# Table rows of chunk 0 loaded in the projection, its tables made on VectorE, and the last yc store awaited in the recurrence

## What is computed

```python
def decay_matrix(G):
    c = G.shape[-1]
    mask = jnp.tril(jnp.ones((c, c), bool))
    return jnp.exp(jnp.where(mask, G[..., :, None] - G[..., None, :], -jnp.inf))
# gdn_chunked
    A = jnp.eye(c) + jnp.einsum('bnhid,bnhjd->bnhij', kb, k) * dec * strict
    qk = jnp.einsum('bnhid,bnhjd->bnhij', q, k) * dec
# ssd_chunked
    cb = jnp.einsum('bnhis,bnhjs->bnhij', Ch, Bh) * dec
```

## Time and profile before

| | us |
|---|---|
| timed runs | 1489.11, 1484.39, 1483.92 |
| median | 1484.39 |
| the profiled execution, whole | 1489.36 |
| its span, first to last instruction | 1487.7 |
| TensorE busy in the span | 1350.8 (91%) |
| VectorE / ScalarE / Gpsimd busy | 930.3 / 638.4 / 312.4 |
| stretch 492 to 538, end of the projection: TensorE busy | 45.13 of 46 |
| stretch 538 to 815, recurrence: TensorE busy | 248.91 of 277 |

### The profile page before, as it was taken

How to read it: one execution, slowest core, us unless ns; L and a number is a source line. 1 busy time by engine, 2 the same in 40 slices (tenths; PEclk the granted TensorE clock), 3 DMA queues, 4 the chain that set the end, 5 groups by cost and what they waited for, 6 DMA issues and landing times. The chain is left out here.

```text
span 1487.7 us, 22400 instructions
## 1 busy us (share of the span) xinstructions
PE 1350.8 (91%) x8237; PEld 1212.4 (81%) x8237; DVE 930.3 (63%) x1310; ACT 638.4 (43%) x960; POOL 312.4 (21%) x329
## 2 busy tenths in 40 slices
PE   7999999999999958999998869999938999999990
PEld 5999999999999958989998648888726888788870
DVE  4579666611245325757776756455268999899973
ACT  6331211222120014435443343333225888888874
POOL 0011111100000024735461100000002333333320
PEclk9999999999999988989999759999967999999995
DMA  5011122222211046263441655432244988889938
GB/s 214 29 43 42 43 73 88 88 96 88 74 58 57 32 103 175 59 132 65 97 79 50 244 186 188 128 118 69 70 187 139 265 267 268 266 276 277 281 57 286
DMA packets 118685, 199.22 MB, mean 134 GB/s; under 512 B 64412, under 2 KB 89244, under 8 KB 113732
## 3 DMA queue, kind: packets, MB, share of 16 engines
q1 hardware_dynamic: 103028, 140.70, 30.6%
q0 software_dynamic: 15568, 57.37, 13.8%
HBM read 202.12 MB, written 49.41 MB: 169 GB/s over the span
## 5 line engine op out<-in xcount | busy, mean ns | idle before, releaser
L98 PE MATMUL c_ps<-hn_lo,c_whi 128*128 128x368 f32 x936 | 177.5, 332 | 0.0
L98 PE MATMUL c_ps<-hn_hi,c_wlo 128*128 128x368 f32 x936 | 176.7, 331 | 0.0
L98 PE MATMUL c_ps<-hn_hi,c_whi 128*128 128x368 f32 x936 | 176.7, 331 | 0.0
L2305 DVE TENSOR_TENSOR e_winlo<-e_win,e_winhi 128x2048 fp32r<-128x2048 f32 x66 | 151.2, 2292 | 20.8 <-ACT e_winhi L2233 18.5
L98 PEld LDWEIGHTS c_ps<-hn_lo,c_whi 128*128 128x128 f32 x936 | 159.4, 188 | 4.8 <-issue 4.8
L98 PEld LDWEIGHTS c_ps<-hn_hi,c_wlo 128*128 128x128 f32 x936 | 159.9, 188 | 0.0
L98 PEld LDWEIGHTS c_ps<-hn_hi,c_whi 128*128 128x128 f32 x936 | 159.9, 188 | 0.0
L82 ACT CAST c_whi<-c_w 128x1024 fp32r<-128x1024 f32 x40 | 42.0, 1050 | 216.6 <-PE c_ps L98 216.6
L2233 ACT CAST e_winhi<-e_win 128x2048 fp32r (+1 forms) x66 | 122.7, 1915 | 4.0 <-DMA e_win<-in_w_gate_up 2.9
L2146 POOL DMA_INDIRECT x_rows<-e_ys,idx_out x33 | 82.1, 2489 | 147.1 <-ACT e_ys L2258 147.1
L597 DVE SCALAR_TENSOR_TENSOR c_y<-c_raw,c_taps,c_y 128x1128 f32<-128x1128 f32 x60 | 83.7, 1394 | 7.0 <-DVE c_y L593 2.1
(11 more groups left out here) (497 smaller groups left out, 2713.8 us busy)
## 6 DMA issues: line engine op xcount, KB each, us to landing
e_win<-in_w_gate_up SPq DMA_DIRECT2D x33, 2048.0 KB
e_wdn<-in_w_down SPq DMA_DIRECT2D x33, 1024.0 KB
c_w<-in_w_in SPq DMA_DIRECT2D x40, 512.0 KB, 3.5
rc_eb<-g_rows SPq DMA_DIRECT2D x10, 1040.0 KB, 5.9
o_land<-in_w_out SPq DMA_DIRECT2D x8, 768.0 KB, 6.7
x_rows<-o_land POOLq DMA_DIRECT2D x12, 512.0 KB, 4.6
rc_gb<-g_rows SPq DMA_DIRECT2D x10, 507.0 KB
kv<-in_xT SPq DMA_DIRECT2D x4, 1104.0 KB, 9.7
```

What stands on the lines that cost most here:

```text
L98: mm = pe.matmul(dst, left(x, k), right(z, k), start=(n == 0 and k == 0), stop=(n == 2 and k == ks - 1))
L2305: dve.tensor_tensor(win_r[1][:, r % 2, ks, :], landed(win, here)[:, ks, :], win_r[0][:, r % 2, ks, :].bitcast(F32), ALU.subtract).then_inc ...
```

## The change

Three things are moved.

1. A new object, `Across`, holds memory and semaphores that live through both the projection and the recurrence. Its buffer `near` is the projection's weight buffer, and, on its first 104 partitions, the recurrence's buffer of table rows. SyncE loads chunk 0's table rows into it in the projection, once the last weights have been split. The three gate rows in SBUF now live only through the projection.
2. Chunk 0's tables are made by VectorE instead of Gpsimd, between its mask constants and its clears; the bodies of `gdn_tables` and `ssd_tables` are the same and count on the same semaphore. Tables of later chunks stay on Gpsimd. TensorE's wait for VectorE's nine settings moves down, to the product of the keys with the state.
3. The last yc block is sent without a wait behind it, and the history store goes out ahead of it. The wait for the last yc stores is now the last thing on SyncE's list in the recurrence.

```diff
 # projection_phase
-        w = m.sb("c_w", [P, 2, KD, P])
+        w, out, out_sent = across.weights, across.out, across.out_sent
-        out = m.sb("c_out", [P, 2, T])
...
                 # SyncE, after the stores of the gate rows
                 sp.wait_ge(gates.out, 64)
                 for h in range(2):
-                    sp.wait_ge(out_sent[h], 16 * (I_C - I_X + NC // 2))
+                    sp.wait_ge(lo_done[h], NB_ALL // 2)
+                across.load_gg(sp, g_dram, 0)
+                across.load_gs(sp, g_dram, 0)
                 sp.wait_ge(kept, 32)
...
                     # Gpsimd, for b in range(NC)
+                    if b == NC - 1:
+                        pool.wait_ge(ctail_done, NC + 1)
+                        pool.dma_start(io["new_hist_c"], tails_c[:]).then_inc(kept, 16)
                     pool.wait_ge(yc_done, b + 2)
-                    send(yc_dram[b:b + 1], b % 2, 16 * (I_C - I_X + b // 2 + 1))
-                pool.wait_ge(ctail_done, NC + 1)
-                pool.dma_start(io["new_hist_c"], tails_c[:]).then_inc(kept, 16)
+                    if b < NC - 1:
+                        send(yc_dram[b:b + 1], b % 2, 16 * (I_C - I_X + b // 2 + 1))
+                    else:
+                        pool.dma_start(yc_dram[b:b + 1].rearrange("a p t -> (a p) t"), out[:, b % 2, :]
+                                       ).then_inc(out_sent[b % 2], 16)

+class Across:
+
+    def __init__(self, m):
+        self.near = m.sb("near", [P, (NROWS - R_SSD) * CH])
+        self.out = m.sb("c_out", [P, 2, T])
+        self.gg_loaded, self.gs_loaded = m.sem("rc_gg"), m.sem("rc_gs")
+        self.out_sent = [m.sem(f"c_sent{h}") for h in range(2)]
+        self.weights = self.near[:, 0:2 * KD * P].rearrange("p (h k c) -> p h k c", h=2, k=KD)
+        self.tables = self.near[0:CH].rearrange("p (r t) -> p r t", t=CH)
+
+    def load_gs(self, sp, g_dram, c):
+        sp.dma_start(self.tables[:, 0:R_Q - R_SSD], g_dram[R_SSD:R_Q, c * CH:(c + 1) * CH].partition_broadcast(CH)
+                     ).then_inc(self.gs_loaded, 16)
+
+    def load_gg(self, sp, g_dram, c):
+        sp.dma_start(self.tables[:, R_Q - R_SSD:], g_dram[R_Q:, c * CH:(c + 1) * CH].partition_broadcast(CH)
+                     ).then_inc(self.gg_loaded, 16)

 # recurrence_phase
-        gb, eb = sb("gb", [L, NROWS - R_SSD, L]), sb("eb", [P, R_B, L])
+        gb, eb = across.tables, sb("eb", [P, R_B, L])
...
             # SyncE
-            load_gg(0)
-            load_gs(0)
             load_x(slice(0, CH), near_loaded, near_loaded)
             load_eb(0)
...
             sp.wait_ge(moved, 32)
+            for h in range(2):
+                sp.wait_ge(across.out_sent[h], 16 * ((NZ + NC) // 2 + (NCONV - NQKV) // 2))
...
             # gdn_tables and ssd_tables: bodies as before, with the engine and its wait as arguments
             # Gpsimd
             pool.wait_ge(dve_set, 9)
-            gdn_tables(0)
-            ssd_tables(0)
             pool.wait_ge(b_loaded, 16)
...
             for c in range(1, NCH):
-                gdn_tables(c)
-                ssd_tables(c)
+                gdn_tables(pool, wait, c)
+                ssd_tables(pool, wait, c)
                 decay(c - 1)
...
             # VectorE, after the six mask constants
+            dve.wait_ge(dve_set, 6)
+            gdn_tables(dve, wait, 0)
+            ssd_tables(dve, wait, 0)
             dve.memset(eps[:], DK * EPS).then_inc(dve_set, 1)
...
                 # TensorE
                 wait(v, c - 1, "s1")
-                if c == 0:
-                    pe.wait_ge(dve_set, 9)
                 products(sq_(QK, HA), kc, qc, all_heads).then_inc(p.sem, 1)
...
                 wait(a, c, "m8_1")
+                if c == 0:
+                    pe.wait_ge(dve_set, 9)
                 products(wide(K, HA), kg, S, all_heads).then_inc(p.sem, 1)

 # program
-                rows = [mi.sb(f"rows_{i}", [P, T]) for i in "abc"]
-                columns = Columns(mi, "col", CH, NCH)
+                columns, across = Columns(mi, "col", CH, NCH), Across(mi)
                 with ExitStack() as first:
+                    rows = [Memory(nc, first).sb(f"rows_{i}", [P, T]) for i in "abc"]
```

More of the change, by code:

```diff
@@ L260, in keep_tail, with projection_phase @@
     return eng.tensor_copy(tail[:, 1:, :], samples(raw, hist_n + TP, hist_n + LSEQ, LSEQ, hist_n + LSEQ))
-def projection_phase(nc, io, hn, gates, q, kv, rows, columns, last_columns, ones, masks, xbc_dram, z_dram, yc_dram, g_dram):
+def projection_phase(nc, io, hn, gates, q, kv, rows, columns, last_columns, ones, masks, xbc_dram, z_dram, yc_dram, g_dram, across):
     with ExitStack() as stack:
         m = Memory(nc, stack)
-        w = m.sb("c_w", [P, 2, KD, P])
+        w, out, out_sent = across.weights, across.out, across.out_sent
         w_r = [m.sb(f"c_w{x}", [P, 2, KD, P], F32R) for x in ("hi", "lo")]
@@ L311, in projection_phase @@
         tapped, conv_done, silu_done = pair("tapped"), pair("conv"), pair("silu")
-        z_done, out_sent, out_free = pair("z"), pair("sent"), pair("outfree")
+        z_done, out_free = pair("z"), pair("outfree")
         h_done, craw_done, ctapped, yc_done = m.sem("c_h"), m.sem("c_craw"), m.sem("c_ctapped"), m.sem("c_yc")
@@ L757, with recurrence_phase @@
 REC_POOL = ["q", "t", "qm", "tm", "d", "doff", "d16", "s", "sm"]
-def recurrence_phase(nc, io, qkv, x, bcs, columns, last_columns, ahead, late, g_dram, masks, xbc_dram):
+def recurrence_phase(nc, io, qkv, x, bcs, columns, last_columns, ahead, late, g_dram, masks, xbc_dram, across):
     L, HP, HPG = CH, HA // 2, HB // GB
@@ L781, in recurrence_phase @@
         decayed = m.sem("rc_decayed")
-        gs_loaded, gg_loaded, eb_loaded = m.sem("rc_gs"), m.sem("rc_gg"), m.sem("rc_ebl")
+        gs_loaded, gg_loaded, eb_loaded = across.gs_loaded, across.gg_loaded, m.sem("rc_ebl")
         x_loaded, b_loaded, moved = m.sem("rc_xl"), m.sem("rc_bl"), m.sem("rc_moved")
@@ L858, in load_gs @@
                 wait(q, c - 1, "s")
-                sp.dma_start(gb_s, g_dram[R_SSD:R_Q, c * CH:(c + 1) * CH].partition_broadcast(L)
-                             ).then_inc(gs_loaded, 16)
+                across.load_gs(sp, g_dram, c)
             def load_gg(c):
                 wait(q, c - 1, "d")
-                sp.dma_start(gb[:, HB:], g_dram[R_Q:, c * CH:(c + 1) * CH].partition_broadcast(L)
-                             ).then_inc(gg_loaded, 16)
+                across.load_gg(sp, g_dram, c)
             def load_eb(c):
@@ L896, in _, with gdn_tables, ssd_tables @@
             sp.wait_ge(moved, 32)
+            for h in range(2):
+                sp.wait_ge(across.out_sent[h], 16 * ((NZ + NC) // 2 + (NCONV - NQKV) // 2))
+        def gdn_tables(eng, wait, c):
+            col = columns.of(c)
+            wait(v, c - 1, "lm")
+            wait(v, c - 1, "qkt")
+            eng.wait_ge(gg_loaded, 16 * (c + 1))
+            eng.tensor_tensor(dec_q, gb_q, bc(col["sub"], L), ALU.subtract).then_inc(q.sem, 1)
+            eng.tensor_tensor(dec_k, gb_k, bc(col["sub"], L), ALU.subtract).then_inc(q.sem, 1)
+            wait(q, c, "q")
+            eng.tensor_tensor(dec_q, dec_q, over(neg_t, HA), ALU.add).then_inc(q.sem, 1)
+            wait(q, c, "t")
+            eng.tensor_tensor(dec_k, dec_k, over(neg16_t[:], HA), ALU.add).then_inc(q.sem, 1)
+            eng.tensor_tensor(dec_16, bc(col["add"], L), gb_b, ALU.subtract).then_inc(q.sem, 1)
+            wait(q, c, "d")
+            eng.tensor_tensor(dec_off, dec_16, over(neg_off[:], HA), ALU.add).then_inc(q.sem, 1)
+            eng.tensor_tensor(dec_16, dec_16, over(neg16[:], HA), ALU.add).then_inc(q.sem, 1)
+        def ssd_tables(eng, wait, c):
+            wait(v, c - 1, "cbt")
+            eng.wait_ge(gs_loaded, 16 * (c + 1))
+            eng.tensor_tensor(dec_s, gb_s, bc(columns.of(c)["ssd"], L), ALU.subtract).then_inc(q.sem, 1)
+            wait(q, c, "s")
+            eng.tensor_tensor(dec_s, dec_s, over(neg_t, HB), ALU.add).then_inc(q.sem, 1)
         @block.gpsimd
@@ L900, in _ @@
             wait = waiter(pool)
[L902 to L925, removed]
             def decay(c):
@@ L2522, in program @@
                     projection_phase(nc, io, hn, gates, q, kv, rows, columns, last_columns, ones, masks, xbc_dram, z_dram, yc_dram,
-                                     g_dram)
+                                     g_dram, across)
                 x = right.sb("x", [P, 4, T])
@@ L2528, in program @@
                 bcs = mi.sb("bcs", [P, 4, T])
-                recurrence_phase(nc, io, (q, k, v), x, bcs, columns, last_columns, ahead, late, g_dram, masks, xbc_dram)
+                recurrence_phase(nc, io, (q, k, v), x, bcs, columns, last_columns, ahead, late, g_dram, masks, xbc_dram, across)
             mixing = Mixing(Memory(nc, mixers), io, z_dram, yc_dram)
```

## The result

| | before | changed |
|---|---|---|
| runs, median us | 1484.16 (4 runs, 1483.79 to 1489.11) | 1475.66 (4 runs, 1473.88 to 1477.62) |
| changed to before, with 95% interval | | 0.9941 [0.9927, 0.9956] |
| the profiled execution, whole / its span | 1489.36 / 1487.7 | 1476.02 / 1474.3 |

What follows compares the result with a forecast made beforehand. The prediction took chunk 0 to end by a chain of transfers and then Gpsimd's work; 3.8 us from the earlier start plus 5.0 from the table loads gave 1484.4 - 8.8 = 1475.6 us, range 1471.0 to 1481.0.

Steps and rivals of the forecast that it cites:

- What bounds: Chunk 0 of the recurrence ends by a chain of transfers, then 13.06 us of Gpsimd; speeding VectorE alone does not help.
- The seam: Between projection and recurrence: without waiting for the last yc block, the recurrence starts 3.8 us earlier (bounds 2.1 to 4.5).
- The queue: Head of the recurrence's load queue: moving chunk 0's table loads (0.865 MB) into the projection saves 5.0 us (3.4 to 6.3).
- rival A: Recurrence's far loads go out sooner, up to 1.5 us more; at most 12.3 us gained, 1472.1; chance 0.12.
- rival B: Smaller gain from start and loads: 5.5 us, 1478.9, or only 3.8 if SyncE's issuing paces far loads; chance 0.23.
- VectorE: Chunk 0's tables take 6.4 us on VectorE; first masked product 9.5 us earlier, but nothing counted beyond the transfers' gain.
- the sum: Chunk 1's table rows land 3.8 + 5.0 = 8.8 us earlier, and all behind them runs as before, 8.8 us earlier.
- Rival C: TensorE stands still up to 10 us in chunk 0; clock 0.50 through chunk 1 adds about 13 us, 1488.6; chance 0.05.
- border of 7.4 us: For the whole kernel, about 0.5%, the smallest difference a measurement can tell from no change; faster means below 1477.0.

Runs made afterwards that it cites:

- the first four experiments: Changed kernel with, in turn: last yc store moved into the recurrence, 1477.20 us; tables back on Gpsimd, 1477.67; table loads back, 1483.02; old projection end back, 1478.84.

## Why the prediction was right, and by which of its steps

*What bounds: right.* Chunk 0 ended by the chain of transfers and Gpsimd. Shorten the queue and the end moves with it (4.5 to 4.9 us for 0.865 MB); speed up VectorE alone and it doesn't move; take the queue out of Gpsimd's way and chunk 0 falls from 34 to 26. That VectorE's speed is worth nothing stands on the trace; the medians leave room for some 2 us.

*The seam: mis-sized.* "with the barrier's 0.9 us as they are now the block starts at 538.5, 3.8 us earlier" took the barrier for the cost and the store for free. It is the other way round: the barrier is 0.26 and the store holds the block, 4.23 us from its issue; in the kernel before Gpsimd saw such a store landed 3.57 us after the issue (535.77 to 539.34), so the hold lasts some 0.7 beyond that. The prediction's lower bound for this term described that case and gave 2.1; 2.1 to 2.4 were measured. A row that could have warned stood there: once SyncE had seen the history store land, the barrier still took 0.9 us, and without a store of Gpsimd's in flight it takes 0.26.

*The queue: right,* 4.9 against 5.0, and for the reason given. Nothing of rival A's further 1.5 us came: far bcs landed no earlier than the bytes account for. What spoke for rival B, that whatever goes first in a block is slow, is refuted by the first stretch of the changed kernel's recurrence, from 540.8 to 546.6: without table rows it runs at 233 GB/s, where the one with them, as far behind its start, had 174. The table rows themselves are slow, also in the projection, where they now travel alone at 172 GB/s (the two stretches are the columns of the earlier trace rows):

```profile
513.00:518.00 5.00, 5.00 (x32) 5.00 (x31) 0.00 (x0) 0.00 (x0) 0.00 (x0) 1.00 0.90 172
...
540.80:546.60 5.80, 3.18 (x18) 2.92 (x16) 5.70 (x11) 3.17 (x7) 0.00 (x0) 0.72 0.94 233
```

*VectorE: right that it is off the path,* and 0.7 us faster than counted.

*What made up for the seam.* The missing 1.5 us came back in two places that the sum had at nothing: 0.3 in the wait for chunk 1's table rows and 1.0 behind Gpsimd's start. Of this 1.0, 0.8 lie between VectorE's SSD state sum and the next first product, 582.23 - 576.12 = 6.11 us against 590.88 - 583.94 = 6.94. The cause is the clock's slow stretch, now over by 578, while before it lay wholly behind that sum (0.50 from 586 to 588). In all four kernels with one part put back or moved (the first four experiments) the clock is back at 1.00 within the first microsecond of this piece, and it takes 5.28 or 5.29 us; here it is in the run with the seam back:

```profile
579.99:585.27 5.28, 5.28 (x50) 5.18 (x49) 2.95 (x7) 1.60 (x6) 0.00 (x0) 1.00 0.93 213
```

No run changes the clock alone, but the length of the piece follows it in these six traces. The prediction had none of this, so the exact hit of the total is partly luck.

*Rival C: its mechanism came, its price did not.* TensorE did stand still (5.08 us, up to 10 forecast) and its clock fell, but for some 6 us within chunk 0, most of it ahead of a chain that waited anyway and only the last 2 us on the chain; chunk 1 took 23.94. The Trainium skill's warning of idle gaps in a loop (TensorE: Matmul & The Clock Gate, on the gate's oscillation) fits that fall; the clock was back by 578. The prediction gives no row for its 13 us for a whole chunk. In chunk 3 of the kernel before the clock is low for the last 8 us and the chunk 4.3 us longer than in the changed kernel; at that price a whole chunk would cost, an estimate, 13 (23.9 x 4.3 / 8). Two thirds of that would only have cancelled the gain and not, as the prediction says, have made the kernel slower by more than its border of 7.4. In chunk 3 the same thing does cost time, by up to 6 us, and the prediction rightly left those 5.0 us of the profiled execution out of the sum without knowing their place.

*Open.* Why the clock falls in chunk 3 in some executions and not in others; why chunk 0 still takes 1.4 to 2.1 us longer than chunk 1 of the changed kernel once the queue is out of its way; what VectorE's tables are worth, between nothing and some 2 us; and the 2 to 3 us by which the median of the kernel with the loads back exceeds its trace's account.

## What to carry to other kernels

Find the chain that ends the stretch, then price each edit by how far it moves that chain: nine instructions on an engine one and a half to almost two times as fast were worth nothing by the trace, two loads taken out of the head of a queue were worth 5 us. A broadcast load that nobody needs soon should not stand in the queue ahead of one that starts a chain; it is worth looking for such loads in every chunk, not only at the seam. Before a wait at a block's end is removed, look at what else is still in flight there: the block may wait for it all the same.

## What the runs showed of the hardware

- A store of 552 KB issued by Gpsimd and awaited by no instruction still held the end of the block: the next block began 4.23 to 4.24 us after its issue, and 0.26 us after the last compute instruction where no such store was in flight. Behind the 36 KB of the history store, for which SyncE waited, it began 2.97 to 3.00 us after the issue.
- TensorE's granted clock fell from 1.00 to 0.50 after a standstill of 5.08 us and stayed there for some 6 us of further products; the piece that follows took 6.94, 6.11 or 5.28 us, as more, less or nothing of such a slow stretch lay in it.
- The same subtraction of 104x416 took 0.58 us on VectorE and 0.88 on Gpsimd, the additions of a mask 0.58 and 1.05; of 104x832, 1.02 against 1.57 and 1.95.
- Table rows spread over 104 partitions held up what lay behind them in the queue by 4.5 to 4.9 us for 0.865 MB, while the loads that took their place ran at 233 GB/s.
